# A hybrid decoder block on one core: six modulation columns summed in the attention steps in place of the merge stage

## The reference, cut to what matters

```python
c_act = jax.nn.silu(c)                                   # c: (1, 1024)
mod = c_act @ w_ada[0] + b_ada[0]                        # 1024 -> 6 * 1024
shift1, scale1, gate1, shift2, scale2, gate2 = jnp.split(mod, 6, axis=-1)
h = modulate(rmsnorm(x, g_norm1), shift1, scale1)        # x: (1, 512, 1024)
z = h @ w_in[0]                                          # -> xr, gr, q, k, v, fl, mg
y_rnn = gelu(gr) * rg_lru(conv(xr))
y_attn = forgetting_attention(q, k, v, log_sigmoid(fl + b_fgate))   # 8 heads of 128
g_r, g_a = jnp.split(jax.nn.sigmoid(mg), 2, axis=-1)
merged = g_r * (y_rnn @ w_proj_rnn) + g_a * (y_attn @ w_proj_attn)
x = x + gate1 * (merged @ w_out)
h = modulate(rmsnorm(x, g_norm2), shift2, scale2)
x = x + gate2 * (convffn(h))                             # d_ff = 3072
return modulate(rmsnorm(x, g_final), shift_f, scale_f)   # c_act @ w_ada_final
```

## Time and profile before

| What | Value |
|---|---|
| Median of 3 runs | 1019.55 us (1019.28 to 1019.68) |
| Profiled execution: its time, its span | 1018.75 us, 1017.0 us |
| TensorE busy | 985.3 us, 97% of the span |
| VectorE busy | 650.8 us, 64% |
| ScalarE busy | 401.4 us, 39% |
| GpSimd busy | 60.1 us, 6% |
| DMA | 130.85 MB, mean 129 GB/s |
| Granted TensorE clock, mean | 0.991 of full speed |
| Mean of ScalarE's `hi` L565 | 1.762 us |
| Mean of VectorE's `lo` L905 | 2.247 us |
| Mean of a sum L917 | 0.752 us, 84 of them |

### The profile page before, as it was taken

The page is one execution under the profiler, slowest core; times in us unless marked ns, Lnnn a source line. Parts: engine busy times, 40 slices in busy tenths (PEclk is TensorE's granted clock), DMA queues, the critical chain, the costliest instruction groups (busy, mean ns, idle before and its releaser), DMA issues.

```text
span 1017.0 us, 12730 instructions
## 1 busy us (share of the span) xinstructions
PE 985.3 (97%) x4629; PEld 810.7 (80%) x4629; DVE 650.8 (64%) x831; ACT 401.4 (39%) x501; POOL 60.1 (6%) x41
## 2 busy tenths in 40 slices
PE   7789999899999999999999999999999999999997
PEld 3468888578889898888888887888888888888875
DVE  2798999899953637363655536667775344655565
ACT  4157777622233626363532335322232232332241
POOL 0111222411100000000000001000000000000000
PEclk9989999999999999999999999999999999999999
DMA  9723221477652321222233227556542323223302
GB/s 338 281 69 94 93 93 41 155 239 243 189 187 84 104 83 63 85 100 82 83 132 116 82 84 248 166 167 205 165 165 91 116 82 104 94 92 109 139 6 78
DMA packets 107384, 130.85 MB, mean 129 GB/s; under 512 B 4588, under 2 KB 85204, under 8 KB 106972
## 3 DMA queue, kind: packets, MB, share of 16 engines
q1 hardware_dynamic: 105392, 126.12, 37.4%
q10 hardware_dynamic: 1964, 4.35, 1.2%
HBM read 126.25 MB, written 4.21 MB: 128 GB/s over the span
## 4 chain that ended last, share of the span: by engine, by line
PE 77%; DVE 14%; issue 4%; DMA 2%; ACT 2%; DVEq 0%; ACTq 0%; SPq 0%
PE ps L1451 25%; PE ps L1453 24%; PE ps L1452 24%; DVE wsplit L905 3%; DMA ada_first<-in_w_ada 2%; DVE xc L1032 2%; DVE ada_acc L917 2%; PE ps L1491 1%; PE ps L1651 1%; DVE th L1071 1%; DVE ig L1069 1%; DVE yrnn L1076 1%; DVE yrnn L1078 1%; DVE mod L949 0%; DVE h L1015 0%
## 5 line engine op out<-in xcount | busy, mean ns | idle before, releaser
L1451 PE MATMUL ps<-h,wsplit 128*128 128x512 f32 x864 | 340.5, 394 | 10.7 <-DVE h L1015 6.1
L1452 PE MATMUL ps<-h,wsplit 128*128 128x512 f32 x864 | 337.7, 391 | 0.0
L1453 PE MATMUL ps<-h,wsplit 128*128 128x512 f32 x864 | 337.7, 391 | 0.0
L905 DVE TENSOR_TENSOR wsplit<-wraw,wsplit 128x2048 fp32r<-128x2048 f32 (+1 forms) x75 | 168.5, 2247 | 69.9 <-ACT wsplit L846 37.2
L1451 PEld LDWEIGHTS ps<-h,wsplit 128*128 128x128 f32 x864 | 163.1, 189 | 46.8 <-issue 4.6
L1453 PEld LDWEIGHTS ps<-h,wsplit 128*128 128x128 f32 x864 | 163.1, 189 | 34.3
L1452 PEld LDWEIGHTS ps<-h,wsplit 128*128 128x128 f32 x864 | 163.3, 189 | 33.1
L565 ACT ACTIVATE wsplit<-wraw 128x2048 fp32r<-128x2048 f32 (+1 forms) x74 | 130.4, 1762 | 142.4 <-PE ps L1453 124.6
L1379 DVE SCALAR_TENSOR_TENSOR cv<-ps,vec,cv 128x511 f32<-128x511 f32 (+1 forms) x48 | 35.8, 748 | 51.9 <-ACT cv L862 48.7
L917 DVE SCALAR_TENSOR_TENSOR ada_acc<-ada_raw,small,ada_acc 128x512 f32<-128x512 f32 x84 | 63.2, 752 | 3.0
L1451 PE MATMUL ps<-wsplit,act_s 128*128 128x512 f32 x160 | 62.3, 389 | 0.7 <-DVE act_s L1366 0.7
(11 more groups left out here) (237 smaller groups left out, 1369.0 us busy)
## 6 DMA issues: line engine op xcount, KB each, us to landing
wraw<-in_w_in SPq DMA_DIRECT2D x26, 1024.0 KB, 5.0
wraw<-in_w_ffn_up SPq DMA_DIRECT2D x24, 1024.0 KB, 5.2
ada_raw<-in_w_ada SPq DMA_DIRECT2D x16, 1024.0 KB, 5.2
wraw<-in_w_ffn_down SPq DMA_DIRECT2D x10, 1024.0 KB, 4.8
ada_first<-in_w_ada SPq DMA_DIRECT2D x8, 1024.0 KB, 16.8
ada_raw<-in_w_ada_final SPq DMA_DIRECT2D x8, 1024.0 KB, 5.1
wraw<-in_w_proj_rnn SPq DMA_DIRECT2D x8, 640.0 KB, 4.4
wraw<-in_w_in SPq DMA_DIRECT2D x8, 512.0 KB, 3.6
```

The source lines that it names most:

```text
L905: ve.tensor_tensor(wsplit[:, s, LO, 0:n], wraw[:, s, 0:n], wsplit[:, s, HI, 0:n].bitcast(F), ALU.subtract).then_inc(w_lo, 1)
L1451: te.matmul(dst, lhs(LO), rhs(HI), start=start, stop=False)
L1452: te.matmul(dst, lhs(HI), rhs(LO), start=False, stop=False)
L1453: return te.matmul(dst, lhs(HI), rhs(HI), start=False, stop=stop)
```

## The change

Columns 4 to 9 leave the merge loop. Two each are done in attention steps 0, 1 and 2, in buffers of their own (`ada2_raw`, `ada2_acc`, `ada2_split`, `ada2_diag`) and in PSUM bank 7. The sums of a column are cut into pieces that stand between the other operations of VectorE. The last column's `ada_store` is in step 3, which is unrolled out of the loop, on VectorE and on TensorE; SP's loop is unrolled whole. `weighted(i, 0)`, which writes bank 7, waits in addition for the `ada_store` before it.

```diff
 # SP
             with sp.Fori(0, KD - 2) as j:
                 load(C_MIX + 2, j, cols_of(w_pr_v, P * j, P), NR, P)
                 load(C_MIX + 3, j, cols_of(w_in_v, COL_MR + 2 * P + P * j, P), KD, P)
-                load_ada(4 + j, cols_of(w_ada_v, 4 * T + T * j, T))
...
             sp.wait_ge(nF_stored, 16)
             load_nF(0)
-            with sp.Fori(4, 2 * H - 3, 4) as i4:
+            load_ada2(4)
+
+            def load_step(i4):
                 load(C_ATT - 1, i4, cols_of(w_in_v, COL_MA - 256 + 64 * i4, 256), KD, 256, 1)
+                load_ada2(i4 // 2 + 3)
                 load(C_ATT, i4, cols_of(w_in_v, COL_Q + 64 * i4, 256), KD, 256, 1)
                 load(C_ATT + 1, i4, cols_of(w_in_v, COL_K + 64 * i4, 256), KD, 256, 1)
                 load(C_ATT + 2, i4, cols_of(w_in_v, COL_V + 64 * i4, 256), KD, 256, 1)
 
                 sp.wait_ge(s_add, 2 * i4)
                 load_nF(i4)
+            for i in range(1, H // 2):
+                load_step(4 * i)
+                if i < H // 2 - 1:
+                    load_ada2(2 * i + 4)
 # VectorE, merge
             with ve.Fori(0, KD - 2) as j:
-                ada(4 + j)
                 gate_product(j, C_MIX + 2, j)
                 ve.wait_ge(w_lo, whole(C_MIX + 3, j))
                 lo(C_MIX + 4, j, NR * P)
-                ada_store(4 + j)
 # VectorE, attention: ada2(idx, k0, k1) does the sums k0 to k1 - 1 of a column
-            def att_step(i):
+            def att_step(i, sums=True):
+                a, b = 2 * i + 4, 2 * i + 5
                 scores_add(i, 0)
                 lo(C_ATT, i, stride=4)
                 probs_norm(i, 0)
                 scores_add(i, 1)
                 probs_norm(i, 1)
+                ada_store(a - 1, 7, ada2_diag if sums else ada2_diag_last)
                 probs_lo(i, 0)
                 lo(C_ATT + 1, i, stride=4)
                 qk_lo(i, 0, 0)
                 y_lo(i, 0)
                 probs_lo(i, 1)
+                if sums:
+                    ada2(a, 0, 4)
                 qk_lo(i, 1, 0)
                 lo(C_ATT + 2, i, stride=4)
                 y_lo(i, 1)
+                if sums:
+                    ada2(a, 4, 7)
                 qk_lo(i, 0, 1)
+                if sums:
+                    ada2(a, 7, 8)
+                    ada2_halves(a)
+                    ada2(b, 0, 3)
                 qk_lo(i, 1, 1)
                 lo(C_ATT + 3, i, stride=4)
+                if sums:
+                    ada_store(a, 7, ada2_diag)
                 v_lo(i, 0)
+                if sums:
+                    ada2(b, 3, 8)
+                    ada2_halves(b)
                 v_lo(i, 1)
 
             lo(C_ATT + 1)
+            ada2(4, 0, 4)
             qk_lo(0, 0, 0)
             qk_lo(0, 1, 0)
             lo(C_ATT + 2)
+            ada2(4, 4, 7)
             qk_lo(0, 0, 1)
+            ada2(4, 7, 8)
+            ada2_halves(4)
+            ada2(5, 0, 3)
             qk_lo(0, 1, 1)
             lo(C_ATT + 3)
+            ada_store(4, 7, ada2_diag)
             v_lo(0, 0)
+            ada2(5, 3, 8)
+            ada2_halves(5)
             v_lo(0, 1)
-            with ve.Fori(1, H // 2) as i:
+            with ve.Fori(1, H // 2 - 1) as i:
                 att_step(i)
+            att_step(H // 2 - 1, sums=False)
 # TensorE, merge: both ada_total(4) and ada_total(4 + j) go; attention:
             def weighted(i, t):
                 te.wait_ge(pt_lo, 6 * (i - 1) + 3 * t + 3)
+                if t == 0:
+                    te.wait_ge(ada_out, min(2 * i + 4, 10) if isinstance(i, int) else 2 * i + 4)
...
                 scores(i, 0)
                 gate_proj(i, 0)
+                ada_total(2 * i + 3, 7, ada2_split)
                 scores(i, 1)
...
                 qk_proj(i, 1, 1)
+                if sums:
+                    te.wait_ge(ya_lo, 2 * i)
+                    ada_total(2 * i + 4, 7, ada2_split)
                 v_proj(i)
...
             te.wait_ge(att_lo, 2)
             qk_proj(0, 1, 1)
+            ada_total(4, 7, ada2_split)
             v_proj(0)
```

More of the change, by code:

```diff
@@ L133, in hybrid_block @@
         merged_a = at("merged_a", 144, [P, KD, T])
+        ada2_acc = at("ada2_acc", 104, [P, T])
+        ada2_diag = at("ada2_diag", 106, [P, T])
+        ada2_diag_last = at("ada2_diag_last", 124, [P, T])
+        ada2_split = at("ada2_split", 108, [P, 2, T], F32R)
+        ada2_raw = [at("ada2_raw0", 120, [P, 4, T]), at("ada2_raw1", 136, [P, 4, T])]
         pt = at("pt", 160, [P, 2, 1280], F32R)
@@ L392, in load, with load_ada, load_ada2 @@
                   .then_inc(w_loaded[s], 16)
-            def load_ada(idx, src):
+            def load_ada(idx, src, raw=(ada_raw[:, 0], ada_raw[:, 1])):
                 for s in range(2):
                     sp.wait_ge(ada_part, 8 * (idx - N_START) + ADA_FIRST + 4 * s - 4)
-                    sp.dma_start(ada_raw[:, s], src[:, 4 * s:4 * s + 4, :]).then_inc(ada_loaded[s], 16)
+                    sp.dma_start(raw[s], src[:, 4 * s:4 * s + 4, :]).then_inc(ada_loaded[s], 16)
+            def load_ada2(idx):
+                load_ada(idx, cols_of(w_ada_v, T * idx, T), (ada2_raw[0][:, :, :], ada2_raw[1][:, :, :]))
             def cols_of(v, col, n):
@@ L918, in ada_sums, with ada_some, ada_halves, ada2 @@
                           .then_inc(ada_part, 1)
-            def ada(idx):
[L921 to L930, removed]
+            def ada_some(idx, k0, k1, raw, acc):
+                before = 8 * (idx - N_START) + ADA_FIRST
+                for k in range(k0, k1):
+                    w = raw[k // 4][:, k % 4]
+                    if k % 4 == 0:
+                        ve.wait_ge(ada_loaded[k // 4], 16 * (idx - N_START) + 16)
+                    if k == 0:
+                        wait_from(ve, ada_hl, 2 * (idx - N_START))
+                        ve.tensor_scalar(acc[:, :], w, cact[:, k:k + 1], None, ALU.mult).then_inc(ada_part, 1)
+                    else:
+                        ve.wait_ge(ada_part, before + k)
+                        ve.scalar_tensor_tensor(acc[:, :], w, cact[:, k:k + 1], acc[:, :], ALU.mult, ALU.add)\
+                          .then_inc(ada_part, 1)
+            def ada_halves(idx, acc, split):
+                ve.wait_ge(ada_mm, idx)
+                ve.wait_ge(ada_part, 8 * (idx - N_START) + ADA_FIRST + 8)
+                ve.tensor_copy(split[:, HI], acc[:, :]).then_inc(ada_hl, 1)
+                ve.wait_ge(ada_hl, 2 * (idx - N_START) + 1)
+                ve.tensor_tensor(split[:, LO], acc[:, :], split[:, HI].bitcast(F), ALU.subtract)\
+                  .then_inc(ada_hl, 1)
+            def ada(idx):
+                ada_some(idx, 0, 8, (ada_raw[:, 0], ada_raw[:, 1]), ada_acc)
+                ada_halves(idx, ada_acc, ada_split)
+            def ada2(idx, k0, k1):
+                ada_some(idx, k0, k1, ada2_raw, ada2_acc)
+            def ada2_halves(idx):
+                ada_halves(idx, ada2_acc, ada2_split)
             def ada_first_sums(acc, quarters, before):
@@ L935, in ada_first_sums, with ada_store @@
                                for q in quarters for k in range(4)], before)
-            def ada_store(idx, bank=6):
+            def ada_store(idx, bank=6, picked=ada_diag):
                 ve.wait_ge(ada_mm, idx + 1)
-                ve.tensor_tensor(ada_diag[:, :].rearrange("p (j n) -> p j n", j=4),
+                ve.tensor_tensor(picked[:, :].rearrange("p (j n) -> p j n", j=4),
                                  ps[:, bank, :].rearrange("p (j n) -> p j n", j=4),
@@ L945, in ada_store @@
                 m = mod[:, ds(4 * idx, 4)]
-                ve.tensor_reduce(m, ada_diag[:, :].rearrange("p (j n) -> p j n", j=4), AX_X, ALU.add)\
+                ve.tensor_reduce(m, picked[:, :].rearrange("p (j n) -> p j n", j=4), AX_X, ALU.add)\
                   .then_inc(ada_sum, 1)
@@ L1477, in project2, with ada_total @@
                             ins.then_inc(tile0 if t == 0 else w_used, 1)
-            def ada_total(idx):
+            def ada_total(idx, bank=6, split=ada_split):
                 te.wait_ge(ada_hl, 2 * (idx - N_START) + 2)
                 te.wait_ge(ada_out, idx)
-                te.matmul(ps[:, 6, :], ones_r[:, :], ada_split[:, LO], start=True, stop=False)
-                te.matmul(ps[:, 6, :], ones_r[:, :], ada_split[:, HI], start=False, stop=True).then_inc(ada_mm, 1)
+                te.matmul(ps[:, bank, :], ones_r[:, :], split[:, LO], start=True, stop=False)
+                te.matmul(ps[:, bank, :], ones_r[:, :], split[:, HI], start=False, stop=True).then_inc(ada_mm, 1)
             def ada_whole(idx, bank, quarters=(0, 1)):
@@ L1583, in _ @@
             gate_mr(C_MIX + 3, 0)
-            ada_total(4)
             with te.Fori(1, KD - 2) as j:
@@ L1589, in _ @@
                 gate_mr(C_MIX + 3, 0, j)
-                ada_total(4 + j)
             te.wait_ge(mixa_done, KD - 2)
@@ L1691, in _ @@
             qk_proj(0, 1, 1)
+            ada_total(4, 7, ada2_split)
             v_proj(0)
```

(3 more changed lines are left out.)

## The result

The changed kernel is slower: 1021.90 us in the median of 13 runs (1020.03 to 1023.2) against 1018.98 us for the kernel before in the same comparison (13 runs, 1018.4 to 1020.2). The ratio is 1.0027, with a 95% interval of 1.0018 to 1.0035. That is 0.3% where the forecast was no change, 1019.3 us, with 1021.5 as its upper end. In this comparison the kernel before was 0.6 us faster than in the three runs on which the forecast was set; measured as a difference, the forecast was -0.3 us and the result is +2.9. The profiled execution took 1022.0 us with a span of 1020.2 us.

A forecast was written before the change was run, and what follows sets the result against it. TensorE, busy 97% of the span, was taken as the bound. Span 1017.0 - 2.6 (holes) - 2.7 + 2.7 (moved matmuls) + 2.3 (step 0) + 0 = 1016.7, forecast 1019.3 us on the median; 8-in-10 range 1017.2 to 1021.5.

The forecast's parts named there:

- the holes: Merge stage: TensorE's waits for `lo` of the next gate weights close, minus 2.6 us (low 1.7).
- The twelve moved matmuls: `ada_total` matmuls leave the merge stage, minus 2.7 us, and return in attention, plus 2.7 us: 0.
- The slots of steps 1 to 3: Attention: VectorE's idle times hold the moved sums, halves and `ada_store`; 0, bounds 0 and 1 us.
- the feared overflow: Rival, attention: full VectorE slots overflow, each of three steps loses 1 us past its cover, 1022.3 us; 7%.
- The 1.8 us "at most" of ScalarE's half: Merge stage: ScalarE's half of a chunk takes at most 1.8 us, so without the sums `lo` is in time.
- The only new wait: Attention step 0: TensorE waits once on `qk_lo` before the K projection, VectorE's first sum being released by a DMA.
- second stall: Attention step 0: none forecast; halves for `ada_total(4)` end at 315.8, TensorE comes to it at 317.8.
- the stall's size: Attention step 0: columns land at 303.2, TensorE restarts at 306.9, not 304.69: 2.2 us, plus 0.1 slow restart.
- a late landing: Rival, step 0: first columns share engines with later loads, stall some 10 us, 1027 us; partly shared, 1022; 10%.
- the clock: Rival, step 0: TensorE's clock falls after the stall, plus 1.7 us, 1021.0 us; 15%.
- The hidden stall: Rival, step 0: columns come earlier or TensorE's wait ends by 305.5; only closed holes count, 1017.0 to 1017.5 us; 13%.

The follow-up runs named there:

- experiment 4: Changed kernel, with the first column's second half and the next gate weights issued only after its first half landed: 1021.40 us, ratio 1.0021 to the kernel before.
- experiments 3 and 5: Changed kernel with 28, then 13 calls of dead matmuls ahead of TensorE's wait in step 0: 1023.84 us (ratio 1.0042) and 1021.35 us (1.0018).
- experiment 8: The kernel before, profiled a second time with no edit: VectorE's row in the second norm 2.48 us, TensorE's wait 2.0 us; span 1019.2 us.
- experiment 2: Changed kernel with the first four sums put behind the two Q readings on VectorE, load left in place: 1017.55 us, ratio 0.9982 to the kernel before.
- experiments 1 and 2: Changed kernel with the first column's loads issued before the V weights (1017.83 us, ratio 0.9982), and the one described under experiment 2.

## Why the prediction was wrong

**Right.** What bounds the kernel, and the holes: minus 2.6 us forecast, 2.7 measured. The twelve moved matmuls cancel. The slots of steps 1 to 3 hold all that was put in them, with no wait of TensorE; the feared overflow did not come. The 1.8 us "at most" of ScalarE's half was a mean over several shapes (a 128x2048 row takes 1.92 us); the holes closed all the same. The only new wait stands where it was forecast, in step 0, on `qk_lo`, with VectorE released by a DMA, and there is no second stall behind it.

**Wrong: the stall's size.** "The load that was issued at 297.99 right behind nF took 5.7 us; the same for the columns gives 303.2." This took a time measured from the issue of a load that had been issued 0.95 us after nF, and counted it from an issue 0.4 us after nF. The load ahead was not done sooner for that. What the row gives is the landing time itself, 303.7, since the engines had the same 1.5 MB to move. That alone makes the stall 2.8 us. With Q's start at 293.67, as the prediction counts, the half landed at 304.6, 1.4 us later than forecast. Of this, 0.5 is that step; nF itself was issued 0.2 later than before; up to 0.4 is sharing with the 2 MB behind (experiment 4); the remaining 0.3 or so is no more than these landings differ from one profile to another. VectorE then took 0.2 us less than its prices said. The prediction had against a late landing that nF took 3.6 us with a load behind it. With the loads issued 0.4 us behind it, nF took 4.6 us (4.3 in experiment 4): at that distance the trace did not bear this out. The stall measured 3.4 us in the first pair of profiles and 3.6 in the second (both kernels profiled again), for the forecast 2.2, and 0.15 of slow restart for the forecast 0.1.

**Wrong: the clock.** Its fall behind the stall was a rival with 15% and stood in the sum at nothing. It fell in both profiles of the changed kernel, after 3.23 and 3.40 us of waiting, for 1.5 and 2.8 us (restart included), and did not in experiment 4, after 2.86 us. It stayed at 1.00 in both kernels in which dead matmuls filled the wait (experiments 3 and 5). These are five profiled executions, so how often it falls behind such a stall stays open, and so does what it costs in the median. By the Trainium skill ("TensorE: Matmul & The Clock Gate", section "What's actually happening") the throttled state is the default and activity releases it; the traces agree: the clock stayed at 1.00 when dead matmuls filled the same wait. The length of the wait alone does not decide: behind the 2.0 us wait of the second norm, which follows small matmuls, the clock was low in seven of nine profiles.

**The sum with the measured terms.** -2.7 + 3.4 + 1.5 = +2.2 us, or -2.7 + 3.6 + 2.8 = +3.7 with stall and clock of the second profiles; the measured ratio's interval is 1.8 to 3.6 us. The 0.9 us of the second norm in the first pair of profiles is scatter between executions (experiment 8) and no part of it. Against experiment 2, which differs by the place of four sums, the ratios give 4.6 us: the stall is 3.4 to 3.6 of it, and what is left, about 1 us, fits the clock but is no more than the uncertainty of the two ratios. The doubt of the prediction pointed the right way; its weights didn't: within 0.2% had 75%, and the two terms that were off both pushed up.

**The hidden stall.** This rival, 1017.0 to 1017.5 us if the wait were gone, is what experiments 1 and 2 made: 1017.8 and 1017.6 us. The first half of the column has only to be asked for earlier, or summed later; the edit as such is then worth 0.2%. What is left of the 2.6 us of closed holes in those runs is 1.8 us, with an interval (1.0 to 2.8 us) that holds it.

## What to carry to other kernels

Work that is moved into an engine's idle time must have its data there, not only its slot: look up which transfer it waits for, when the queue of the issuing engine reaches that transfer, and what the bytes ahead of it need, and take the landing time from the trace as a point in time, not as a duration from another issue. On an in-order engine put such a wait behind what the bounding engine wants next. And price a stall of the matmul engine with the clock behind it: in the two profiles here, 3.4 and 3.6 us of stall carried 1.5 and 2.8 us more. Where a row lasts longer in one execution, look first whether its end has moved at all.

## What the runs showed that I had not expected

The clock's fall belongs to an execution as much as to a program. The same changed kernel lost 1.5 and 2.8 us behind the same stall. In the second norm one program gave a wait of 0.8 us with the clock low before it, and 2.0 us with the clock low behind it. One profile gives the matmul starts of its own execution; what the clock did in it need not be what it does in the median. VectorE's row in the second norm lasted 1.05 to 2.49 us and yet ended 6.11 to 6.13 us after the `diag` rows began, in every profile. What holds it until then stays open.
